# Expert lists from TensorE, table scatters inside passes 0 and 1, and weight chunks of 16 KB per partition

## The reference, cut to what matters

```python
logits = xt @ router_w + router_b
top_val, top_idx = lax.top_k(logits, 4)
gates = softmax(top_val)
hcat = xb @ w1[e] + b1[e]            # 1024 -> 2048, per expert
h_glu, h_lin = split(hcat); h_glu = min(h_glu, 7); h_lin = clip(h_lin, -7, 7)
act = h_glu * sigmoid(1.702 * h_glu) * (h_lin + 1)
y = act @ w2[e] + b2[e]              # 1024 -> 1024, per expert
h = h + sum over the 4 chosen experts of gate * y
```

## Time and profile before

| | us |
|---|---|
| median of three runs | 1580.52 |
| the profiled execution | 1593.28 |
| its span, first to last instruction | 1591.5 |
| TensorE matmul busy | 1537.9 (97%) |
| VectorE busy | 744.5 (47%) |
| POOL busy | 533.4 (34%) |
| ScalarE busy | 282.6 (18%) |

### The profile page before, as it was taken

The page is one execution under the profiler, slowest core; times in us unless marked ns, Lnnn a source line. Parts: engine busy times, 40 slices in busy tenths (PEclk is TensorE's granted clock), DMA queues, the critical chain, the costliest instruction groups (busy, mean ns, idle before and its releaser), DMA issues.

```text
span 1591.5 us, 38141 instructions
## 1 busy us (share of the span) xinstructions
PE 1537.9 (97%) x15984; PEld 857.2 (54%) x15984; DVE 744.5 (47%) x1563; ACT 282.6 (18%) x406; POOL 533.4 (34%) x689
## 2 busy tenths in 40 slices
PE   7999999999999796999999999999999999999996
PEld 6998988877889532334333333433333343333334
DVE  4799898015242633344335334433533443353367
ACT  5333134346221300001001000100100010010001
POOL 7334333462343445222221222222122222212225
PEclk9999999999999898999999999999999999999998
DMA  7553243221276298999999999999999999999996
GB/s 218 159 181 111 78 144 98 84 75 53 80 291 229 67 334 348 362 417 420 419 418 418 420 418 418 420 418 418 418 419 418 416 421 419 418 419 420 418 418 248
DMA packets 132020, 492.27 MB, mean 309 GB/s; under 512 B 16301, under 2 KB 74085, under 8 KB 82308
## 3 DMA queue, kind: packets, MB, share of 16 engines
q1 hardware_dynamic: 111892, 463.30, 73.3%
q0 software_dynamic: 10448, 17.26, 3.0%
q10 hardware_dynamic: 9632, 11.03, 2.2%
HBM read 475.46 MB, written 24.87 MB: 314 GB/s over the span
## 4 chain that ended last, share of the span: by engine, by line
PE 89%; POOL 3%; DVE 2%; DMA 2%; issue 1%; ACT 1%; SPq 1%; another core or an unknown queue 1%; POOLq 0%; DVEq 0%; ACTq 0%
PE banks L1613 40%; PE banks L1150 28%; PE banks L1642 19%; DMA stage<-in_w_in_dram 1%; POOL code_of L749 1%; DMA code_of<-slot_table 1%; SPq L464 0%; DMA slot_table<-code,dest 0%; DMA xs<-u_rows,piece_now 0%; PE banks L1509 0%; PE banks L1382 0%; POOL h_res L804 0%; DVE h_res L2174 0%; POOL w_lo L629 0%
## 5 line engine op out<-in xcount | busy, mean ns | idle before, releaser
L1613 PE MATMUL banks<-w_ring,xT 128*32 128x512 f32 x6144 | 668.9, 595 | 20.7 <-DVE xT L2118 14.9
L1613 PEld LDWEIGHTS banks<-w_ring,xT 128*32 128x32 f32 x6144 | 190.2, 110 | 479.8 <-issue 474.2
L1642 PE MATMUL banks<-w_ring,actT 128*32 128x256 f32 x6144 | 338.1, 379 | 0.2
L2096 DVE TENSOR_TENSOR hid<-banks,bias_now 128x512 f32<-128x512 f32 x96 | 63.9, 665 | 470.7 <-PE banks L1613 470.7
L1642 PEld LDWEIGHTS banks<-w_ring,actT 128*32 128x32 f32 x6144 | 189.9, 110 | 156.3 <-issue 20.9
L638 POOL TENSOR_TENSOR w_lo<-stage,w_hi 128x2048 fp32r<-128x2048 f32 x38 | 175.3, 4613 | 258.0 <-ACT w_hi L857 258.0
L697 POOL TENSOR_TENSOR carrier<-carrier 1x1 f32<-1x1 f32 x161 | 32.2, 200 | 578.3 <-DVE y_out L2127 418.1
L1124 ACT ACTIVATE sig<-hid 128x256 f32<-128x256 f32 x96 | 40.0, 417 | 918.8 <-DVE hid L2097 900.8
L1150 PE MATMUL banks<-u_hi,w_hi 128*128 128x264 f32 (+1 forms) x528 | 176.5, 334 | 1.0 <-POOL w_lo L629 1.0
L1150 PE MATMUL banks<-u_hi,w_lo 128*128 128x264 f32 (+1 forms) x528 | 175.0, 331 | 0.0
L1150 PE MATMUL banks<-u_lo,w_hi 128*128 128x264 f32 (+1 forms) x528 | 174.6, 331 | 0.0
(11 more groups left out here) (306 smaller groups left out, 1483.1 us busy)
## 6 DMA issues: line engine op xcount, KB each, us to landing
w_ring<-in_expert_w_dram SPq DMA_DIRECT2D x384, 1024.0 KB
stage<-in_w_in_dram SPq DMA_DIRECT2D x20, 1024.0 KB, 5.2
stage<-in_w_in_dram SPq DMA_DIRECT2D x16, 512.0 KB, 5.7
y_rows<-empty_row ACTq DMA_DIRECT2D x8, 1024.0 KB, 4.9
y_in<-y_rows SPq DMA_DIRECT2D x4, 2048.0 KB, 22.2
stage<-in_conv_pw_w_dram SPq DMA_DIRECT2D x4, 1024.0 KB, 5.2
stage<-in_mlstm_out_w_dram SPq DMA_DIRECT2D x4, 1024.0 KB, 5.2
stage<-in_w_out_dram SPq DMA_DIRECT2D x4, 1024.0 KB, 5.3
```

Source lines behind the costliest of these rows:

```text
L1613: last = nc.tensor.matmul(banks[32 * g:32 * (g + 1), t].rearrange("p (c j) -> p c j", j=64), xT[:, t, k], units, start=k == 0, stop=k == K ...
L1642: last = nc.tensor.matmul(banks[32 * g:32 * (g + 1), 3 + t, 0:GRP], actT[:, t, k], w2_ring[k // 2][:, k % 2, GRP * g:GRP * (g + 1)], start ...
L2096: own(nc.vector.tensor_tensor(hid[:, t], banks[:, t], bias1, ALU.add))
```

## The change

Three things change together.

1. **Lists.** TensorE makes expert 2's list (`in_third`, four more matmuls) and expert 0's rows (`in_slot` by `first_code`, four more) besides expert 1's. VectorE makes `in_third` and `first_code` before it transposes expert 0's rows, and writes the results with 24 small operations into `piece_of` and `row_of`. POOL then gathers for expert 1, stores expert 0 and gathers for expert 2 before it needs the table. The 16 table scatters move between the tiles of these two gathers: 2, 3 and 4 of them behind the three tiles of the first, 2, 2 and 3 behind those of the second. From the third on, each waits until the one two before it has landed. The table is read after that with 4 DMAs (32 partitions of 18 runs) instead of 16. The tiles of the first gather are now paced by pass 0 as the later ones are.
2. **Weights.** The ring has 6 chunks of 2 MB with 16 KB per partition in one run: two k of w1, or four of w2. A chunk is released when its last k is done. The pace of the gathers gets semaphores of its own (`row_turn`).
3. **Channels.** Rows 2p and 2p + 1 of a w1 chunk lie on partition p, so `u2`'s channels are dealt in pairs: 8 operations of 128 elements per tile instead of 4 of 256. Slots lie on partitions in their own order (`SPREAD` is gone). Bias and activation layouts follow (runs of 128 elements instead of 64).

```diff
-RING = 12
-W1C = KT
+RING = 6
+W1C = KT // 2
-RC = DFF * 2
+RC = DFF * 4
@@ load_chunk
-                    src = expert_w1[0, bass.ds(e, 1), P * c:P * (c + 1), :].rearrange("e p (g n) -> p (e g) n", g=2)
+                    src = expert_w1[0, bass.ds(e, 1), 2 * P * c:2 * P * (c + 1), :].rearrange("e (p k) n -> p (e k) n", p=P)
-                    src = expert_w2[0, bass.ds(e, 1), 2 * P * m:2 * P * (m + 1), :].rearrange("e (p k) n -> p (e k) n", p=P)
+                    src = expert_w2[0, bass.ds(e, 1), 4 * P * m:4 * P * (m + 1), :].rearrange("e (p k) n -> p (e k) n", p=P)
@@ POOL
-            nc.gpsimd.iota(slot_no, [[32, TG], [1, SPREAD], [SPREAD, TURNS]], ...)
+            nc.gpsimd.iota(slot_no, [[1, SLOTS]], ...)
                 for t in range(TG):
                     if turn is not None:
-                        pool.wait_ge(ring_used[2 * t], turn)
+                        pool.wait_ge(row_turn[t], turn)
...
+                    if between is not None:
+                        places_out(between[t])
+            def places_out(columns):
+                for m in columns:
+                    pool.wait_ge(dest_made, m // TOPK + 1)
+                    if m > 1:
+                        pool.wait_ge(table_written[m % 2], 16 * (m // 2))
+                    pool.indirect_dma_start(out=table, ..., in_=code[:, m:m + 1], in_offset=None).then_inc(table_written[m % 2], 16)
+            def results_out(n, stored):
+                for t in range(TG):
+                    pool.wait_ge(y_made, n * TG + (t + 2))
+                    carry_wait(1 + t)
+                    pool.indirect_dma_start(out=y_dram, ..., in_=y_out[:, t], ...).then_inc(y_stored, 16)
+                pool.wait_ge(y_stored, stored * (16 * TG))
+                carry_wait(1 + TG)
             pool.wait_ge(tables_made, CG * TG)
-            pool.sem_inc(idx_step, 1)
-            request_rows()
-            for i in range(2, TT):
-                places_out(i)
-            pool.wait_ge(table_written, 16 * TT * TOPK)
+            gather(1, 1, 1, (range(0, 2), range(2, 5), range(5, 9)))
+            pool.wait_ge(tables_made, 2 * CG * TG)
+            nc.gpsimd.tensor_copy(row_now, row_of[:, :, 0]).then_inc(idx_step, 1)
+            pool.wait_ge(idx_step, 3 + TG)
+            pool.wait_ge(y_emptied, 16 * KT)
+            results_out(0, 1)
+            pool.wait_ge(xT_made, 2 * TG)
+            gather(2, 8 + TG, 2, (range(9, 11), range(11, 13), range(13, 16)))
+            for half in table_written:
+                pool.wait_ge(half, 16 * (TT * TOPK // 2))
             for g in range(CG):
-                for b in range(TURNS):
-                    pool.dma_start(code_of[32 * g + b:32 * (g + 1):TURNS], by_turn[b]).then_inc(rows_in, 16)
+                pool.dma_start(code_of[32 * g:32 * (g + 1)], table.rearrange("(x j e) o -> j x (e o)", j=32, e=NE)).then_inc(rows_in, 16)
@@ TensorE, before the passes
+            pe.wait_ge(in_slot_made, 3 * TT + 1)
+            for i in range(TT):
+                last = nc.tensor.matmul(banks[0:SLOTS, SECOND_BANK, 1:2], in_third[:, i], token_no[:, i:i + 1], ...)
+            last.then_inc(place_mm, 1)
+            for i in range(TT):
+                last = nc.tensor.matmul(banks[0:SLOTS, SECOND_BANK, 2:3], in_slot[:, i], first_code[:, i:i + 1], ...)
+            last.then_inc(place_mm, 1)
@@ TensorE, expert
-                        last.then_inc(ring_used[k], 1)
+                        last.then_inc(ring_used[k // 2] if k % 2 else row_turn[k // 2], 1)
@@ VectorE
+                    for b in range(2):
+                        nc.vector.scalar_tensor_tensor(out=u2[...][:, b], in0=of_group(h_res[:, i], g)[:, b], ...)
+            for i in range(TT):
+                slots_of(in_third, i, 2).then_inc(in_slot_made, 1)
+            chain(nc.vector.scalar_tensor_tensor(out=first_codes, in0=expert_f, scalar=0.0, in1=code_no, ...))
+            nc.vector.tensor_reduce(first_code, first_codes, axis=AX.X, op=ALU.add).then_inc(in_slot_made, 1)
-                    nc.vector.tensor_scalar(piece_now[32 * g:32 * (g + 1), t:t + 1], ...)
+            for to, from_cols, at_col in ((piece_of, slice(0, 2), 1), (row_of, slice(2, 3), 0)):
+                for g in range(CG): for t in range(TG): nc.vector.tensor_scalar(to[...], banks[...], ...)
```

More of the change, by code:

```diff
@@ L206, in hybrid_block @@
         chunk = size([P, RC])
-        w1_ring = [at(f"w1_ring{c}", [P, 2, DFF], F32, ring_end - chunk * (c + 1)) for c in range(W1C)]
-        w2_ring = [at(f"w2_ring{c}", [P, 2, D], F32, ring_end - chunk * (W1C + c + 1)) for c in range(RING - W1C)]
+        w1_ring = [at(f"w1_ring{c}", [P, 2, 2 * DFF], F32, ring_end - chunk * (c + 1)) for c in range(W1C)]
+        w2_ring = [at(f"w2_ring{c}", [P, 4, D], F32, ring_end - chunk * (W1C + c + 1)) for c in range(RING - W1C)]
         assert ring_end - chunk * RING >= gates_at + chan
@@ L374, in hybrid_block @@
         xs_in, xT_made, idx_step = sem("xs_in"), sem("xT_made"), sem("idx_step")
+        row_turn = [sem(f"row_turn{t}") for t in range(TG)]
         in_slot_made, rows_mm = sem("in_slot_made"), sem("rows_mm")
@@ L496, in _ @@
             sp.dma_start(h_res, x[0].rearrange("(i p) d -> p i d", p=P)).then_inc(row_bc_in, 16)
-            for c in range(4):
+            for c in range(2):
                 load_chunk(0, c)
@@ L501, in _ @@
             sp.wait_ge(mm_done, pair_tick(PW_PAIR + 1, 8))
-            for c in range(4, 6):
-                load_chunk(0, c)
+            load_chunk(0, 2)
             load_pair(WO_PAIR + 1, lambda s: w_source(WO_PAIR, s, 1))
@@ L507, in _ @@
             sp.wait_ge(mixed, KT)
-            for c in range(6, RING):
+            for c in range(3, RING):
                 load_chunk(0, c)
@@ L550, in load_results @@
                     if i < TT - 1:
-                        for c in range(2 * (TT - 2 - i), 2 * (TT - 2 - i) + 2):
-                            sp.wait_ge(ring_used[c], n + 1)
+                        sp.wait_ge(ring_used[TT - 2 - i], n + 1)
                     sp.dma_start(y_in[i], results[i].rearrange("p (k d) -> p k d", k=TOPK)).then_inc(y_loaded[i], 16)
@@ L815, in of_group @@
         def of_group(rows, g):
-            return rows.rearrange("p (k g j) -> p g k j", g=CG, j=32)[:, g]
+            return rows.rearrange("p (m g j b) -> p g b m j", g=CG, j=32, b=2)[:, g]
         def rows_copied(i, f):
@@ L1602, in _ @@
             last.then_inc(place_mm, 1)
+            pe.wait_ge(in_slot_made, 3 * TT + 1)
+            for i in range(TT):
+                last = nc.tensor.matmul(banks[0:SLOTS, SECOND_BANK, 1:2], in_third[:, i], token_no[:, i:i + 1], start=i == 0, stop=i == TT - 1)
+            last.then_inc(place_mm, 1)
+            for i in range(TT):
+                last = nc.tensor.matmul(banks[0:SLOTS, SECOND_BANK, 2:3], in_slot[:, i], first_code[:, i:i + 1], start=i == 0, stop=i == TT - 1)
+            last.then_inc(place_mm, 1)
             pe.wait_ge(passes_made, 1)
@@ L1611, in hidden @@
                         for g in range(CG):
[L1612 to L1613 removed]
+                            units = w1_ring[k // 2][:, k % 2].rearrange("p (c g j) -> p g c j", g=CG, j=128)[:, g]
+                            last = nc.tensor.matmul(banks[32 * g:32 * (g + 1), t].rearrange("p (c j) -> p c j", j=128),
                                                     xT[:, t, k], units,
@@ L1630, in expert @@
                             last = hidden(k, t)
-                            if t == TG - 1 and k < KT - 1:
-                                last.then_inc(ring_used[k], 1)
+                            if t == TG - 1 and k == KT - LATE:
+                                last.then_inc(ring_used[k // 2], 1)
                         last.then_inc(hid_mm, 1)
@@ L2036, in _ @@
                 slots_of(in_second, i, 1).then_inc(in_slot_made, 1)
+            for i in range(TT):
+                slots_of(in_third, i, 2).then_inc(in_slot_made, 1)
+            chain(nc.vector.scalar_tensor_tensor(out=first_codes, in0=expert_f, scalar=0.0, in1=code_no, op0=ALU.is_equal, op1=ALU.mult))
+            nc.vector.tensor_reduce(first_code, first_codes, axis=AX.X, op=ALU.add).then_inc(in_slot_made, 1)
             for t in range(TG):
@@ L2043, in _ @@
             nc.vector.tensor_tensor(gate_w, best[:, :, 0:TOPK], best[:, :, 0:1].to_broadcast([P, TT, TOPK]), ALU.subtract).then_inc(shifted, 1)
-            dve.wait_ge(place_mm, TT + 2)
-            for g in range(CG):
-                for t in range(TG):
-                    nc.vector.tensor_scalar(piece_now[32 * g:32 * (g + 1), t:t + 1], banks[32 * t:32 * (t + 1), SECOND_BANK, 0:1],
-                                            float(CG), float(g), ALU.mult, ALU.add).then_inc(tables_made, 1)
+            dve.wait_ge(place_mm, TT + 4)
+            for to, from_cols, at_col in ((piece_of, slice(0, 2), 1), (row_of, slice(2, 3), 0)):
+                for g in range(CG):
+                    for t in range(TG):
```

(3 more changed lines are left out.)

98 lines of the change are left out of this document (43 added, 55 removed).

## The result

The changed kernel takes 1593.25 us (median of 4 runs, 1591.22 to 1594.51) against 1580.8 us for the kernel before on the same chip: ratio 1.0075, 95% interval 1.0061 to 1.009, so 12.45 us slower. The time lies in the range of 1565 to 1600, on the side that had the largest chance; the forecast of +2.2 us is 10 us short.

What follows compares the result with a forecast made beforehand. TensorE bounds steady passes (30.96 us), so only the hole can be won. It moves to pass 3 at 663.0; plus 1.5 start and 1.5 cold restart, 666.0 against 663.83: +2.2 us, 1582.7 us, range 1565 to 1600.

Steps and rivals of the forecast that it cites:

- the side that had the largest chance: Whole kernel slower than before: chance 0.45, against 0.28 for the same and 0.27 for faster.
- The mechanism: Passes 2 and 3: the 14.85 us hole leaves pass 2; serial scatter landings open 15.9 us before pass 3.
- the prediction's own signs: Right if no idle before pass 2, 12 to 20 us before pass 3, last scatter issued near 612.
- A: Rival, POOL's transfers: they land later behind 16 KB runs, 2.6 us more each, 24 us in all, 1607; chance 0.17.
- C: Rival, before pass 0: the unknown 5.46 us idle goes, giving 1577.2 us; chance 0.05.
- the price of a link in the series of landings: POOL's queue, passes 0 and 1: 5.9 us from issue to landing of each indirect DMA, whatever the run length.
- Table read: Between last scatter's landing and list operations: 4 DMAs take 12.0 us, bounds 6.0 and 17.9, against 17.9 before.
- Expert 2's rows: Gather before pass 2: third tile issued at 602.9, landing about 5.8 us later, before pass 2 is due at 615.1.
- The start: Ahead of pass 0: smaller `u2` operations, more slot matrices and matmuls cost 1.5 us, bounds 0.2 and 3.6.
- Weights: Weight stream: 16 KB runs and 2 MB chunks asked for one k (2.6 us) later, costed at nothing.
- B: Rival, before pass 3: landings short enough (4.5 us each) that the hole closes, 15.1 us faster, 1565.4; chance 0.10.
- D: Rival, later passes: undealt slots load DMA engines unevenly, so weights come late, 8 us, 1590; chance 0.05.

Runs made afterwards that it cites:

- lists alone: The list part of the change on the weights of the kernel before (12 ring slots of 1 MB, 8 KB runs): 1589.59 us, ratio 1.0058.
- 2 MB slots, 8 KB runs: Kernel before with 6 ring slots of 2 MB, each loaded in 8 KB runs per partition, channels not paired: 1584.0 us, ratio 1.0011.
- weights alone: Kernel before with the weights of the change (6 slots of 2 MB, 16 KB runs, paired channels) and its old lists: 1589.37 us, ratio 1.0051.
- first execution: First profiled execution of the kernel before, nothing changed: 1593.28 us, 12.8 us over its timed runs.
- second profile of before: The kernel before profiled a second time, nothing changed: 1581.02 us; used as the kernel before in all later comparisons.
- scatters free: Changed kernel without the waits among its 16 table scatters: 1586.4 us, ratio 1.0032.

## Why the prediction was right and wrong

**The mechanism was right.** The hole goes from pass 2 to pass 3, the series of landings makes it, and TensorE waits for nothing else. The last scatter is issued at 612.25 (forecast 612.0), and that it fits is luck: 612.0 was counted from a pass 0 at 550.67, and pass 0 starts at 541.90. From its start it is 70.4 us where 61.3 were forecast, 9.0 late. By the prediction's own signs the picture is mixed: the idle before pass 3 is above its 12 to 20 us, and the signs of A (idle before pass 2 too, landings over 8 us: 8.47 and 8.36) and of C (a pass 0 before 550) are there as well.

**The step that failed is the price of a link in the series of landings.** I took 5.9 us for each, "so the wait does not follow the length of a run". Up to expert 0's stores the schedule is 2.0 us late; the last store's landing is 8.47 instead of 5.9, 2.6 us; the second gather's scatters add 4.4 us more. Of these, 2.3 are longer landings (7.19, 6.69 and 6.11 for 5.9), and 2.1 are a term that the schedule put at nothing: behind each landing POOL takes another 0.70 us until the next scatter is issued. So the run length is only a part of it. The *lists alone*, with 8 KB runs, issue the last scatter 66.6 us after the start of pass 0 (608.48 - 541.87), which is 5.3 of the 9.0 us; the 16 KB runs add the other 3.7. The evidence that misled me on them was the 6.6 us at the start of the kernel. The DMA engines were as full there (share 0.99 over 4 to 7 us), but the runs were 4 KB and less; from 4 KB and 8 KB runs I concluded for 16 KB. *2 MB slots, 8 KB runs* beside *weights alone* shows that in the early passes the wait does follow the run.

**Table read.** Forecast 12.0 between bounds of 6.0 and 17.9, measured 633.99 - 619.13 = 14.9. The issue was nearly right (2.8 for 3.2); the landing was not. Fewer transfers didn't land sooner (8.09 for 7.95 us), and the 16 KB runs made it 12.07 instead of 8.17. What remains, 32.7 us from the list to the pass, was 30.0, the last gather landing in 2.65 us instead of 5.80 with the stream nearly at rest.

**Expert 2's rows.** Their gather was 6.5 us later from the start of pass 0 than laid out (58.7 for 52.2) and missed pass 2 by 3.09 us. The forecast had it land before pass 2 was due. And the 11.59 us of pass 1's w2 half, by which pass 3 was due at 647.1 and not 646.1, belonged to the first execution too: in the second it is 10.55.

**The start.** +1.5 us was forecast, +1.25 measured, all of it from the lists: with the weights alone the start is the same (25.86 for 25.85), so the halved `u2` operations cost nothing. Missed was that the thinner work ahead of pass 0 lowers the clock (granted clock 0.60 and 0.54 in its first windows): 22.50 for 20.81 us, 1.7 us.

**Weights.** "I cost this at nothing" was wrong twice: +7.8 us at the hole through POOL's landings, -1.0 to -2.4 us in the end, where the results' loads land after a median of 14.5 us (23.6 in the second profile of before). In the changed kernel, against the lists alone, it is 7.8 more at the two holes, 2.5 less at the end and 1.5 less in the late passes: 3.8, as timed (1593.25 - 1589.59 = 3.7).

**The rivals.** A's mechanism was there, at a smaller price in the end: it asked for 2.6 us more per landing in the whole series and 24 us in all; against the lists alone, the scatters in the chain landed 0.1 to 0.9 us later, expert 0's stores 2.1 and the table 3.9. B is out. C was no rival at all: its 5.46 us were never in the timed runs. That taught me too little: the 12.8 us between the profiled execution and the timed runs stood in the page, and a stall whose releaser is an unknown queue was the first place to look for them. D doesn't occur in the changed kernel (0.4 us over in 27 passes), though its slots are not dealt. It does with 8 KB runs, dealt or not: 0.4 to 2.4 us over where a hole is left (0.4 in the kernel before, 1.5 with 2 MB slots), 4.3 and 5.2 where there is none. So what the runs show is 8 KB runs without a hole as the cause; whether the slot order adds to it isn't shown.

**The sum by the runs.** Forecast for the two holes together: 15.9 + 1.5 after 14.85 + 1.5, +1.0. Measured: 29.4 after 18.8, +10.6. That is the missing 10 us. The clock in pass 0 (+1.7) and the end (-2.4), neither of them forecast, nearly cancel. The lower end of the range by its own bounds is 1582.7 - 5 - 6 - 1.3 = 1570.4, not 1569; nothing hangs on it.

## What to carry to other kernels

When work is moved off the path, list the landings that it now waits for one after another, add what the engine needs between a landing and its next issue (0.70 us here), and price each by a row taken under the same traffic. The wait for the same three stores was 1.2 us with the stream nearly at rest (at 670.21 in the changed kernel, DMA share 0.07), 4.7 to 5.9 behind 8 KB runs, and 5.3 to 11.0 behind 16 KB runs. Then look for an order in which they lie beside the engine that bounds: here the same lists and weights are 12 us slower than the kernel before, or 17 us faster with another order on POOL's queue and no waits among the scatters (taking away the waits alone gave 6.9 us). And ahead of any sum compare the profiled execution with the timed runs; what it has too much must be found in it first.

## What was not expected of the hardware

- Small transfers of POOL's queue behind a full stream of weights: the wait for expert 0's stores is 4.9 to 5.9 us behind 8 KB runs, in all eight profiles. Behind 16 KB runs it is 9.67, 9.75 and 11.02 in three, but 7.55 in the changed kernel and 5.53 in *scatters free*. That for 4 table reads is 7.9 to 8.2 and 11.8 to 12.1 us, that for 16 table reads 8.0 to 8.4 and 16.2.
- In steady passes the same stores mostly wait 4.7 to 5.0 us and 5.3 to 6.2. Why the early passes can cost twice that, at the same full DMA share, was not tried.
- One gain of 16 KB runs mostly hides as long as a hole lets the ring fill: the stream keeps up to the last pass (0.4 us over, against 0.4 to 2.4 with a hole and 4.3 and 5.2 without one behind 8 KB runs). Another doesn't: 2 MB loads of results land in a median of 14.5 to 18.8 us beside 16 KB runs of weights and 23.3 to 24.3 beside 8 KB runs, hole or not.
- Matmuls of one column ahead of pass 0 keep TensorE busy for most of the time (1.62 of 2.00 us in 540 to 542), and the granted clock still falls to 0.60 and 0.54 in the next 4 us, so most of them pass at the lower of its two levels (1.2 GHz, 0.50). With 16 wider matmuls between them it stays at 1.00 (2.4 GHz).
